# Prompt latent attention in a decode-step kernel: from one head per unit of 512 queries to two heads in the two row halves of TensorE's array, units of 256 queries

## The chip, the cores and the metric

The kernel runs on one core of one Trainium2 chip. The metric is the time of one launch on the device, in microseconds (us). TensorE is called PE below, its weight loads PEld, VectorE DVE, ScalarE ACT, GpSimd POOL, and SyncE (which issues most DMAs) SP. Each engine runs its own list of instructions in order, and the lists meet only at semaphores.

## The reference

One inference step of one layer of a hybrid decoder: a combined input projection, then three attention branches (latent, dilated windows, cross-attention to a memory), a SiLU gate and an output projection, for a prompt of 2048 tokens and for 64 sample tokens. The change touches only the latent attention of the prompt:

```python
def mla_prompt(q_lat, q_rope, ckv, krope):
    ...
    def block(args):
        ql, qr, start = args
        s = (jnp.einsum('bqhc,bkc->bhqk', ql, ckv)
             + jnp.einsum('bqhr,bkr->bhqk', qr, krope)) * MLA_SCALE
        qpos = start + jnp.arange(Q_BLOCK)
        p, _ = masked_softmax_stats(s, kpos[None, :] <= qpos[:, None])
        return jnp.einsum('bhqk,bkc->bqhc', p.astype(ckv.dtype), ckv)
```

There are 8 heads; the mask is causal. The kernel computes the same with keys and values expanded for each head: for a query, scores against keys of 64 "nope" numbers of its head and 32 rotary numbers that all heads share, a softmax, and a sum of values of 64 numbers per head. The scores have float32 accuracy.

## The kernel before

The program runs its stages one behind the other, with a barrier between them: input projection, prompt windows and memory, prompt latent projections, **prompt latent attention** (`prompt_latent_attention`, L1242), sample attention, output projection. The stage in question begins with a DMA issue at 764.94 us and its last matmul is at 1275 us.

Work is cut into 32 **units** (h, i): one head and 512 queries, the last 512 of a head first. A unit has four query blocks of 128. For each block the scores against all keys up to the diagonal are made in **score steps** of up to 512 keys (320 in all; `width` gives the keys). The steps of one unit:

- *Score* (L1411). Queries and keys are split into a high and a low part of the fast format (F32R), and three matmuls (hi x hi, hi x lo, lo x hi; L75 to L77 in `mm3`) add into one PSUM bank. Nope and rotary rows lie together, so a matmul uses 96 rows of the array. `scores` has two banks, so score step m waits until DVE has taken out step m-2.
- *Eviction* (L1552, operation at L1568). DVE copies the bank to `probs` with mask and scale, and keeps each row's minimum; behind the last step of a block a small reduce (L1573) gives `bias`.
- *Exponentials* (L1506, L1511). ACT works once over a block's whole row, up to 2048 columns, as soon as `bias` is there. They are issued on ACT when the next block's first score step comes.
- *Turn* (L1437). PE transposes `probs` in pieces of 64 x 128 in both row halves (lanes), two key blocks a turn, into one of two slots of `turned`. It waits until all exponentials of the unit are done. ACT copies lane 0 (L1513, L1519) and DVE lane 1 (L1576, L1583) to `probsT`.
- *Value* (L1453, L1463). Plain float32 matmuls of two key blocks against up to 512 columns of `probsT`, one key block in each column half (64 columns) of the array. A float32 matmul appears as two instructions in the trace. `outs` is double buffered.
- *Keep and back* (L1521, L1466, L1586). ACT copies `outs`, PE transposes it back (four transposes), DVE adds the two halves and scales with the reciprocal of the sums, and SP stores.

The order on PE, and with it on DVE and ACT (all three walk the same list `STEPS`), is fixed ahead by `phases()` and `order()` (L1263 to L1283): the phases are "two turns" and "[back of the unit before] two values" in turn, and before each phase score steps are put in until their share of the work is reached, with a lead of 15 us:

```python
        share = sum(0.705 * width(*s) / CH for s in SCORES) / sum(cost[what] for phase in phases() for what, u, p in phase)
...
            while m < len(SCORES) and (scored < share * (turned + LEAD) or m < unit_end[phase[-1][1]]):
```

`probs` has a buffer for each i, so four units can be in work. POOL splits the queries and keys of later units (L1386, L1394), and SP loads them ahead.

## Time and profile before

| | us |
|---|---|
| median of 3 runs (lowest, highest) | 2174.52 (2167.16, 2178.09) |
| the profiled execution's own time | 2173.66 |
| its span | 2172.0 |
| PE busy over the span | 2001.7 (92%) |
| DVE, ACT, POOL busy | 1132.3, 948.9, 416.6 |
| latent attention: first and last matmul start | 770.8, 1275.1 |

The span is the time between the first and the last instruction that the profiler saw; the execution's own time is that of the whole launch. Busy times are sums over instructions, and overlapping instructions of one engine count once. The ends of matmuls are modelled, so a start says more than an end.

### The profile page before, as it was taken

How to read it: one execution, taken by the hardware profiler on the slowest of the kernel's cores; microseconds unless marked ns; L12 is line 12 of the kernel's file. 1: busy time of each engine (PE TensorE's matmuls, PEld its weight loads, DVE VectorE, ACT ScalarE, POOL GpSimd, SP SyncE). 2: the span in 40 equal slices, each digit the busy share in tenths (PEclk: the TensorE clock that was granted, in tenths of full speed). 3: DMA queues.
4: the chain of work that ended last, by engine and by line, in shares of the span. 5: the costliest groups of instructions: out<-in, count | busy, mean ns of one | idle time of the engine just before them, and what ended most of it. 6: DMA issues, size and time to landing. Idle time of an engine off the chain costs nothing. (4 is left out here: it accounts for less than half of the span.)

```text
span 2172.0 us, 45434 instructions
## 1 busy us (share of the span) xinstructions
PE 2001.7 (92%) x16456; PEld 1470.0 (68%) x16456; DVE 1132.3 (52%) x3298; ACT 948.9 (44%) x2124; POOL 416.6 (19%) x530
## 2 busy tenths in 40 slices
PE   6999999688779979999999969999999969999998
PEld 5888887456557745555565545666666658888886
DVE  4333333577864357676776645555555663233222
ACT  4333332578752235555555434444444444243332
POOL 0111111344550022222221112222222100000000
PEclk9999999899999959999999989999999989999999
DMA  8333332623454321111110049877777353233231
GB/s 280 106 113 109 101 116 71 197 83 111 143 142 142 131 68 33 29 35 29 35 33 22 18 119 286 242 228 223 226 229 245 122 191 117 87 89 104 77 106 49
DMA packets 180293, 265.35 MB, mean 122 GB/s; under 512 B 44488, under 2 KB 138776, under 8 KB 171144
## 3 DMA queue, kind: packets, MB, share of 16 engines
q1 hardware_dynamic: 160712, 165.87, 27.1%
q0 software_dynamic: 19424, 97.35, 13.3%
q8 instruction: 102, 1.67, 0.3%
q14 instruction: 55, 0.45, 0.1%
HBM read 210.24 MB, written 52.66 MB: 121 GB/s over the span
## 5 line engine op out<-in xcount | busy, mean ns | idle before, releaser
L75 PE MATMUL proj_acc<-proj_w_hi,proj_x_hi 128*128 128x512 f32 (+2 forms) x544 | 197.6, 363 | 19.0 <-DVE proj_x_lo L299 12.4
L1511 ACT ACTIVATE mla_probs<-mla_probs,mla_bias 128x256 f32<-128x256 f32 (+14 forms) x128 | 154.7, 1209 | 109.2 <-DVE mla_bias L1573 104.5
L76 PE MATMUL proj_acc<-proj_w_lo,proj_x_hi 128*128 128x512 f32 (+2 forms) x544 | 195.9, 360 | 0.0
L77 PE MATMUL proj_acc<-proj_w_hi,proj_x_lo 128*128 128x512 f32 (+2 forms) x544 | 195.3, 359 | 0.0
L1568 DVE CUSTOM_DVE_ANT_0 mla_probs<-mla_scores,mla_zero 128x512 f32<-128x512 f32 x192 | 132.6, 692 | 112.0 <-PE mla_scores L77 108.1
L75 PE MATMUL mla_scores<-mla_k_hi,mla_q_hi 96*128 96x512 f32 (+3 forms) x320 | 143.4, 448 | 30.3 <-DVE mla_lowest L1568 14.5
L1463 PE MATMUL mla_outs<-mla_probsT,prompt_val 128*64 128x512 f32 (+3 forms) x640 | 141.1, 544 | 1.8 <-DVE mla_probsT L1583 1.8
L75 PEld LDWEIGHTS mla_scores<-mla_k_hi,mla_q_hi 96*128 96x128 f32 x320 | 62.5, 195 | 109.6 <-issue 62.6
L1917 PE MATMUL dec_outs<-late_ckv,dec_pT 128*64 128x256 f32 x1024 | 126.5, 389 | 3.7 <-DVE dec_pT L2047 3.7
L75 PEld LDWEIGHTS proj_acc<-proj_w_hi,proj_x_hi 128*128 128x128 f32 x544 | 104.0, 191 | 32.1 <-DVE proj_x_lo L299 12.4
L1862 PE MATMUL dec_scores<-dec_keysT,sample_q_lat 128*64 128x512 f32 x512 | 123.3, 601 | 2.2 <-DVE dec_krT L2025 1.2
L800 ACT ACTIVATE win_probs<-win_probs,win_bias 128x256 f32<-128x256 f32 (+1 forms) x256 | 117.4, 462 | 16.9 <-DVE win_bias L839 16.4
L76 PE MATMUL mla_scores<-mla_k_lo,mla_q_hi 96*128 96x512 f32 (+3 forms) x320 | 122.2, 382 | 0.0
L77 PE MATMUL mla_scores<-mla_k_hi,mla_q_lo 96*128 96x512 f32 (+3 forms) x320 | 121.8, 381 | 0.0
L353 DVE COPY proj_featT<-proj_tr 128x512 f32<-128x512 f32 x34 | 23.5, 692 | 187.8 <-PE proj_tr L406 186.0
L75 PE MATMUL fin_gate<-fin_wg_hi,fin_x_hi 128*128 128x512 f32 x272 | 109.0, 401 | 11.8 <-DVE fin_wg_lo L2340 8.1
L2047 DVE COPY dec_pT<-dec_p_turned 128x256 f32<-128x256 f32 x80 | 34.0, 424 | 159.7 <-PE dec_outs L1878 130.4
L1803 POOL DMA_INDIRECT late_ckv<-in_cache_ckv,sample_rows_of x63 | 59.8, 950 | 291.1 <-PE dec_outs L1917 278.6
L1519 ACT ACTIVATE mla_probsT<-mla_turned 128x512 f32<-128x512 f32 (+1 forms) x160 | 80.0, 551 | 79.4 <-PE mla_turned L1449 79.3
L77 PEld LDWEIGHTS proj_acc<-proj_w_hi,proj_x_lo 128*128 128x128 f32 x544 | 103.8, 191 | 12.9
L76 PEld LDWEIGHTS proj_acc<-proj_w_lo,proj_x_hi 128*128 128x128 f32 x544 | 103.8, 191 | 11.8
L77 PE MATMUL fin_gate<-fin_wg_hi,fin_x_lo 128*128 128x512 f32 x272 | 107.4, 395 | 0.0
(354 smaller groups left out, 4617.8 us busy)
## 6 DMA issues: line engine op xcount, KB each, us to landing
win_v_tile<-wv_out SPq DMA_DIRECT2D x75, 128.0 KB
proj_x_raw<-in_xT SPq DMA_DIRECT2D x17, 512.0 KB, 3.9
proj_rows<-in_x SPq DMA_DIRECT2D x17, 512.0 KB, 5.3
featT<-proj_featT POOLq DMA_DIRECT2D x34, 256.0 KB, 2.8
late_ckv<-in_xT SPq DMA_DIRECT2D x17, 512.0 KB, 6.8
fin_mix<-mix SPq DMA_DIRECT2D x17, 512.0 KB, 3.6
late_ckv<-in_x SPq DMA_DIRECT2D x17, 512.0 KB, 3.8
y_out<-late_ckv POOLq DMA_DIRECT2D x17, 512.0 KB, 6.5
```

What stands on the lines that cost most here:

```text
L75: pe.matmul(out, lh, rh, start=start, stop=False)
L76: pe.matmul(out, lh, rl, start=False, stop=False)
L77: return pe.matmul(out, ll, rh, start=False, stop=stop)
L800: e = act.activation(pr, pr, ACT.Exp, bias=bias[:, u, h:h + 1], scale=ATT_SCALE, accum_out=rec[:, q, 0, 256 + H_B + h:256 + H_B + h + 1])
L1463: mm = pe.matmul(outs[64 * kb:64 * kb + 64, u % 2, q0:], val[:, at, h, :], probsT[:, g % 2, kb, q0:], start=p == 0, stop=p == PAIRS[u] - 1)
L1511: act.activation(row, row, ACT.Exp, bias=bias[:, b_:b_ + 1], scale=-1.0, accum_out=total[:, b_:b_ + 1]).then_inc(exp_done, 1)
L1519: act.activation(dst, src, ACT.Copy).then_inc(turned_act, 1)
L1568: dve.tensor_tensor_reduce(probs[i][:, j, c * CH:c * CH + n], scores[:, m % 2, 0:n], add, -MLA_SCALE, -LOWEST, ALU.add, ALU.min, low).then ...
L1803: pool.indirect_dma_start(ckv[:, u, :, :].rearrange("p m c -> p (m c)"), None, ckv_rows, rows).then_inc(ckv_loaded[u], 16)
L1862: pe.matmul(scores[h * Q:(h + 1) * Q, u, :], q_lat[:, c, s, :], keysT[:, u, c, h * 512:(h + 1) * 512], start=c == 0, stop=False)
L1917: mm = pe.matmul(outs[h * Q:(h + 1) * Q, 0:KVL], pT[:, u, j, h * Q:(h + 1) * Q], values[:, h * HALF + j, :], start=j == 0, stop=j == HALF - 1)
L2047: dve.tensor_copy(pT[:, n % 2, :, 0:Q], halves_turned[0]).then_inc(pT_dve, 1)
```

## The change

Units are now (m, i): a **pair of heads** and **256 queries**, 32 in all; i runs up for even m and down for odd m. A score step serves both heads of the pair and there are 160. Head 2m lies in array rows 0 to 63, head 2m+1 in rows 64 to 127, so a step's matmuls use 64 rows each and come in pairs, one for each half. The shared rotary part no longer fits beside the nope part; it is packed as 32 rows of high and 32 rows of low part (`kr_parts`), with the rotary queries held twice. A step has five matmuls per head in place of three. `scores` has three banks, taken in turn by the heads of the steps. `probs` holds two units of any size. A value step has both heads on the column halves, two key blocks one behind the other, in one bank `outs` that is not double buffered any more; so `finish` needs no addition. The lead is 10 us and never more than one unit. The exponentials of both heads of a block are issued together. Loads have three DMAs for a unit's queries in place of two, and key chunks 1 to 3 of the first pair are split by ACT and DVE at units 1, 2 and 4. The core of the diff:

```diff
-    SB = 4
-    CH = SB * P
-    UNITS = [(h, i) for h in range(H_A) for i in reversed(range(SEQ // CH))]
+    QB = 2
+    CW = QB * P
+    CH = 512
+    NI = SEQ // CW
+    UNITS = [(m, i) for m in range(H_A // 2) for i in (range(NI) if m % 2 == 0 else reversed(range(NI)))]
     NU = len(UNITS)
-    LEAD = 15.0
+    LEAD = 10.0
...
+    STEPS_OF_SCORES = [(u, j, c) for u, (m, i) in enumerate(UNITS) for j in range(QB) for c in range(chunks(i, j))]
+    SCORES = [(u, j, c, s) for u, j, c in STEPS_OF_SCORES for s in range(2)]
+    PAIRS = [i + 1 for m, i in UNITS]
...
+        cost = {"turn": 0.58, "value": 0.95, "back": 0.25}
+        share = (sum(score_cost(k) for k in range(len(STEPS_OF_SCORES)))
+                 / sum(cost[what] for phase in phases() for what, u, p in phase))
+        k, scored, turned = 0, 0.0, 0.0
         for phase in phases():
-            turned += sum(cost[what] for what, u, p in phase)
-            while m < len(SCORES) and (scored < share * (turned + LEAD) or m < unit_end[phase[-1][1]]):
-                yield ("score", m, 0)
-                scored += 0.705 * width(*SCORES[m]) / CH
-                m += 1
+            u = phase[-1][1]
+            turned += sum(cost[what] for what, a, p in phase)
+            while k < len(STEPS_OF_SCORES) and k < unit_end[min(u + 1, NU - 1)] and (scored < share * (turned + LEAD) or k <= unit_end[u]):
+                yield ("score", k, 0)
+                scored += score_cost(k)
+                k += 1
             yield from phase
...
+        kr_parts = b.sb("kr_parts", [P, SEQ], F32R)
+        lower = b.sb("lower", [P, 1])
+        probs = b.sb("probs", [P, 2, 2 * QB, SEQ])
         probsT = b.sb("probsT", [P, 2, 2, CH])
-        outT = b.sb("outT", [P, 2, CH])
-        both = b.sb("both", [P, 2, SB, VH])
-        out = b.sb("out", [P, 2, SB, VH])
-        mask = b.sb("mask", [P, CH + P])
+        outT = b.sb("outT", [P, 2, CW])
...
-        scores = b.ps("scores", [P, 2, CH])
+        NR = NU * QB * 2
+        lowest = b.sb("lowest", [P, NR, SEQ // CH])
+        bias = b.sb("bias", [P, NR])
+        total = b.sb("total", [P, NR])
+        inv = b.sb("inv", [P, NR])
+        scores = b.ps("scores", [P, 3, CH])
         turned = b.ps("turned", [P, 2, 2, CH])
-        outs = b.ps("outs", [P, 2, CH])
+        outs = b.ps("outs", [P, CH])
...
+                parts = ((qn_hi[:, u % 2, mine], k_hi[:, m % 2, cols]), (qr_hi[:, u % 2, mine], kr_parts[:, cols]),
+                         (qn_hi[:, u % 2, mine], k_lo[:, m % 2, cols]), (qn_lo[:, u % 2, mine], k_hi[:, m % 2, cols]),
+                         (qr_lo[:, u % 2, mine], kr_parts[:, cols]))
+                for a, (lhs, rhs) in enumerate(parts):
+                    for s in range(2):
+                        at = 2 * k + s
+                        if a == 0 and at >= 3:
+                            pe.wait_ge(masked, at - 2)
+                        rows = slice(64 * s, 64 * s + 64)
+                        mm = pe.matmul(scores[:, at % 3, 0:n], lhs[rows, :], rhs[rows, :], start=a == 0, stop=a == len(parts) - 1)
+                        if a == len(parts) - 1:
+                            mm.then_inc(scores_done, 1)
...
+                pe.wait_ge(exp_done, 2 * QB * (u + 1))
...
-                if p == 0 and u >= 2:
-                    pe.wait_ge(out_kept, u - 1)
+                if p == 0 and u:
+                    pe.wait_ge(out_kept, u)
                 for kb in range(2):
                     at = 2 * p + kb
-                    q0 = max(0, at - SB * i) * P if i or at > 1 else 0
-                    mm = pe.matmul(outs[64 * kb:64 * kb + 64, u % 2, q0:], val[:, at, h, :], probsT[:, g % 2, kb, q0:], start=p == 0, stop=p == PAIRS[u] - 1)
+                    q0 = max(0, at - QB * i) * P
+                    for s in range(2):
+                        mm = pe.matmul(outs[64 * s:64 * s + 64, q0:CW], val[:, at, 2 * m + s, :],
+                                       probsT[:, g % 2, kb, s * CW + q0:(s + 1) * CW], start=at == 0, stop=at == 2 * PAIRS[u] - 1)
                 mm.then_inc(pv_done, 1)
...
-                for j in range(SB):
+                for j in range(QB):
...
+                    for s in range(2):
+                        if c == 0 and (u or j):
+                            exponentials(*((u, j - 1, s) if j else (u - 1, QB - 1, s)))
+                    if a == len(STEPS_OF_SCORES) - 1:
+                        for s in range(2):
+                            exponentials(u, j, s)
...
-                halves = turned[:, r % 2, 0, :].rearrange("p (j b d) -> p j b d", j=SB, b=2)
-                dve.tensor_copy(both[:, u % 2, :, :], halves[:, :, 0, :]).then_inc(added, 1)
-                dve.wait_ge(added, u + 1)
-                dve.tensor_tensor(both[:, u % 2, :, :], both[:, u % 2, :, :], halves[:, :, 1, :], ALU.add).then_inc(turned_dve, 1)
-                dve.wait_ge(turned_dve, r + 1)
-                dve.wait_ge(inverted, u + 1)
                 if u >= 2:
                     dve.wait_ge(stored[u % 2], 16 * (u // 2))
-                dve.tensor_tensor(out[:, u % 2, :, :], both[:, u % 2, :, :], inv[:, s].rearrange("p (j o) -> p j o", o=1).broadcast_to([P, SB, VH]), ALU.mult).then_inc(result_done, 1)
+                dve.tensor_tensor(out[:, u % 2, :, :, :].rearrange("p j s d -> p (j s) d"),
+                                  turned[:, r % 2, 0, 0:QB * P].rearrange("p (w d) -> p w d", d=VH),
+                                  inv[:, rows].rearrange("p (w o) -> p w o", o=1).broadcast_to([P, 2 * QB, VH]), ALU.mult).then_inc(turned_dve, 1)
```

Two places of the changed order. On **PE**, around the end of a unit's scores (in `scores` step order; `mla_turned<-mla_ident,mla_probs` are the turns). Before, 512 queries of one head:

```order
L1449 MATMUL mla_turned<-mla_ident,mla_probs 128x64 x32
L75 MATMUL mla_scores<-mla_k_hi,mla_q_hi 128x512
L76 MATMUL mla_scores<-mla_k_lo,mla_q_hi 128x512
L77 MATMUL mla_scores<-mla_k_hi,mla_q_lo 128x512
L75 MATMUL mla_scores<-mla_k_hi,mla_q_hi 128x384
L76 MATMUL mla_scores<-mla_k_lo,mla_q_hi 128x384
L77 MATMUL mla_scores<-mla_k_hi,mla_q_lo 128x384
L1471 MATMUL mla_turned<-mla_ident,mla_outT 128x128 x4
L1463 MATMUL mla_outs<-mla_probsT,prompt_val 64x512 x4
```

Now, the last score step of unit 9 (pair 1, i = 6, 256 keys), the first of unit 10 (512 keys), and the first turns of unit 9:

```order
L1474 MATMUL mla_scores<-mla_k_hi,mla_qn_lo 128x256 x2
L1474 MATMUL mla_scores<-mla_kr_parts,mla_qr_lo 128x256 x2
L1474 MATMUL mla_scores<-mla_k_hi,mla_qn_hi 128x512 x2
L1474 MATMUL mla_scores<-mla_kr_parts,mla_qr_hi 128x512 x2
L1474 MATMUL mla_scores<-mla_k_lo,mla_qn_hi 128x512 x2
L1474 MATMUL mla_scores<-mla_k_hi,mla_qn_lo 128x512 x2
L1474 MATMUL mla_scores<-mla_kr_parts,mla_qr_lo 128x512 x2
L1501 MATMUL mla_turned<-mla_ident,mla_probs 128x64 x32
L1525 MATMUL mla_turned<-mla_ident,mla_outT 128x128 x2
L1516 MATMUL mla_outs<-mla_probsT,prompt_val 64x256 x8
```

Scores stood between turns and values; here they stand ahead of the turns, and the turns of a unit follow one score step behind that unit's own last scores.

On **ACT**, the exponentials (`mla_probs,mla_total`) and the copies (`mla_probsT`). Before, around the longest row:

```order
L1511 ACTIVATE mla_probs,mla_total<-mla_probs,mla_bias 128x2048
L1519 ACTIVATE mla_probsT<-mla_turned 128x8x64
L1519 ACTIVATE mla_probsT<-mla_turned 128x2x2x64
L1511 ACTIVATE mla_probs,mla_total<-mla_probs,mla_bias 128x1152
L1525 ACTIVATE mla_outT<-mla_outs 128x512
```

Now, units 6 and 7 (i = 6 and 7 of pair 0):

```order
L1556 ACTIVATE mla_probs,mla_total<-mla_probs,mla_bias 128x1792 x2
L1564 ACTIVATE mla_probsT<-mla_turned 128x8x64 x4
L1556 ACTIVATE mla_probs,mla_total<-mla_probs,mla_bias 128x1920 x2
L1564 ACTIVATE mla_probsT<-mla_turned 128x8x64 x3
L1570 ACTIVATE mla_outT<-mla_outs 128x256
L1556 ACTIVATE mla_probs,mla_total<-mla_probs,mla_bias 128x2048 x2
L1564 ACTIVATE mla_probsT<-mla_turned 128x8x64 x6
```

One exponential at a time has become two in a row, and the copies behind the pair of 2048 columns are those of the unit to which that pair belongs.

## Rows read from the trace of the kernel before

**Rows 1.** Page, busy us of each engine over the span

```profile
PE 2001.7 (92%) x16456; PEld 1470.0 (68%) x16456; DVE 1132.3 (52%) x3298; ACT 948.9 (44%) x2124; POOL 416.6 (19%) x530
```

**Rows 2.** Stretches of the stage: busy us of PE, PEld, DVE, ACT, POOL; PEclk; DMA share; GB/s

```profile
770.70:806.40 35.70, 31.53 (x103) 22.32 (x104) 21.34 (x57) 14.89 (x18) 11.11 (x12) 0.50 0.20 52
785.00:795.00 10.00, 10.00 (x24) 6.82 (x24) 5.84 (x17) 4.66 (x4) 3.09 (x4) 0.50 0.00 0
850.00:1250.00 400.00, 387.44 (x3227) 238.05 (x3225) 282.42 (x846) 213.23 (x368) 86.45 (x92) 1.00 0.12 29
```

**Rows 3.** PE timeline of the stage: start us, length us, engine, line, tiles, shapes, count

```profile
1000.64 1.94 PE L1463 MATMUL mla_outs<-mla_probsT,prompt_val 128*64 128x512 f32 x8
1002.51 0.50 PE L75 MATMUL mla_scores<-mla_k_hi,mla_q_hi 96*128 96x512 f32 x1
1002.85 0.40 PE L76 MATMUL mla_scores<-mla_k_lo,mla_q_hi 96*128 96x512 f32 x1
1003.08 0.39 PE L77 MATMUL mla_scores<-mla_k_hi,mla_q_lo 96*128 96x512 f32 x1
1003.40 0.84 PE L1449 MATMUL mla_turned<-mla_ident,mla_probs 64*128 64x64 f32 x20
```

**Rows 4.** PE timeline in the windows stage (row halves of 64)

```profile
541.74 1.13 PE L735 MATMUL win_scores<-win_k_tile,win_q_tile 64*128 64x256 f32 x8
542.80 1.09 PE L751 MATMUL win_outs<-win_probsT,win_v_tile 128*64 128x128 f32 x16
```

**Rows 5.** PE timeline in the decode stage (column halves of 64)

```profile
1603.46 1.95 PE L1917 MATMUL dec_outs<-dec_v_rows,dec_pT 128*64 128x256 f32 x16
1605.24 1.89 PE L1862 MATMUL dec_scores<-dec_keysT,sample_q_lat 128*64 128x512 f32 x8
1606.95 1.04 PE L1866 MATMUL dec_scores<-dec_krT,sample_q_rot 128*64 128x128 f32 x16
```

**Rows 6.** Timeline around one eviction that the next scores wait for

```profile
858.61 0.40 PE L77 MATMUL mla_scores<-mla_k_hi,mla_q_lo 96*128 96x512 f32 x1
859.19 0.69 DVE L1568 CUSTOM_DVE_ANT_0 mla_probs<-mla_scores,mla_zero 128x512 f32<-128x512 f32 x1
859.81 0.28 DVE L1568 CUSTOM_DVE_ANT_0 mla_probs<-mla_scores,mla_mask 128x128 f32<-128x128 f32 x1
859.95 0.51 PE L75 MATMUL mla_scores<-mla_k_hi,mla_q_hi 96*128 96x512 f32 x1 [0.66 <-DVE mla_lowest L1568]
860.14 0.16 DVE L1573 TENSOR_REDUCE mla_bias<-mla_lowest 128x1 f32<-128x3 f32 x1
860.33 1.26 ACT L1511 ACTIVATE mla_probs<-mla_probs,mla_bias 128x1152 f32<-128x1152 f32 x1 [0.55 <-DVE mla_bias L1573]
```

**Rows 7.** Timeline, one exponential of 2048 columns and what follows on ACT

```profile
856.93 1.99 ACT L1511 ACTIVATE mla_probs<-mla_probs,mla_bias 128x2048 f32<-128x2048 f32 x1
858.92 0.86 ACT L1519 ACTIVATE mla_probsT<-mla_turned 128x512 f32<-128x512 f32 x2
```

**Rows 8.** Timeline of the stage's end: turns, copies, values, one back

```profile
1257.41 1.22 PE L1449 MATMUL mla_turned<-mla_ident,mla_probs 64*128 64x64 f32 x32
1258.16 1.29 DVE L1583 COPY mla_probsT<-mla_turned 128x512 f32<-128x512 f32 x2 [0.55 <-PE mla_turned L1449]
1259.00 1.94 PE L1463 MATMUL mla_outs<-mla_probsT,prompt_val 128*64 128x512 f32 x8 [0.38 <-DVE mla_probsT L1583]
1265.40 0.63 PE L1471 MATMUL mla_turned<-mla_ident,mla_outT 128*128 128x128 f32 x4 [0.37 <-DVE mla_probsT L1583]
```

**Rows 9.** Waits in the stage, turns for exponentials: us, times, longest

```profile
PEld mla_turned L1449 <- ACT mla_probs L1511: 0.8, 1, 0.8
```

**Rows 10.** Two stretches of the windows stage, one behind the other

```profile
437.80:441.30 3.50, 1.09 (x16) 0.88 (x16) 3.43 (x19) 2.14 (x9) 1.75 (x4) 1.00 0.14 44
441.30:444.70 3.40, 3.32 (x26) 2.44 (x26) 2.00 (x8) 2.37 (x9) 2.70 (x5) 0.50 0.09 30
```

**Rows 11.** Weight loads of one score group, PEld timeline

```profile
1002.61 0.19 PEld L76 LDWEIGHTS mla_scores<-mla_k_lo,mla_q_hi 96*128 96x128 f32 x1
```

More of the change, by code:

```diff
@@ L1360, in store @@
[L1360 to L1368 removed]
+                m, i = UNITS[u]
```

318 lines of the change are left out of this document (162 added, 156 removed).

## The prediction

> **What bounds the kernel now.** I read the page's busy times first: PE is busy for 2001.7 us of 2172.0, the next engine (DVE) for 1132.3 [rows 1]. Then the stretches of the one stage that the change touches: over 400 us of its middle PE is busy for 387.44, DVE for 282.42, ACT for 213.23, at a granted clock of 1.00 [rows 2]. So PE sets the pace there and what counts is PE's list: the length of its work and the gaps in it. From the first matmul to 806.40 us the granted clock is 0.50 (1.2 of 2.4 GHz), although PE was busy for all of 785 to 795 [rows 2]. The stage's PE time is 505 us (770.7 to 1276). Behind it come other stages that the change leaves alone, so a change of this time is the change of the kernel's.
>
> The 505 us add up as follows, which tests the prices used below. Scores: 140,288 key columns (the widths of the 320 steps) by three matmuls at 2400 columns/us are 175 us; a 512-column matmul starts 0.23 us behind the last (1002.85 to 1003.08 [rows 3]), 0.017 more than its columns, times 960: 16. Entering and leaving a group of score steps costs 0.11 + 0.09 us (first start to second 0.34, last to the turn 0.32 [rows 3]), times 150 groups: 30. Values: 80 phases of two at about 1.87 (1000.64 to 1002.51 [rows 3]), less for the diagonal ones, 130. Turns: 2192 transposes at 0.038 (1.22 us for 32 [rows 8]), 83. Backs: 32 at some 0.55 [rows 8], 17. That is 451; runs of three and more score steps, the slow clock at the start and the end's waits make up the rest.
>
> **What the change takes away on PE.**
> - Scores: 69,632 columns a head pair, five matmuls: 348,160 columns are 145 us if the two halves run side by side, and 800 pairs by 0.017 are 14. Together 159 in place of 192: **-33**. That the halves do run together rests on the nearest rows: in the windows stage eight instructions with 64 rows and 256 columns (four float32 matmuls, each two instructions of two passes, 0.213 us each) fill 1.06 us, 541.74 to 542.80 [rows 4], not the 1.70 that they need one by one; and less 0.16 for the change of shape, 0.225 us a pair.
> - Groups of score steps: 101 in place of 150, by 0.20: **-10**. Here the scores have the same 64-row shape as the turns, and all 101 groups touch a turn on one side. The extra 0.09 towards a turn was seen with a change from 96 to 64 rows [rows 3]; no row has the new pairing, so that side costs between 0 and 0.09, in all 9 us less or nothing less. I take 0.09, the row, and keep -9 as an end. The page TensorEngine Tiling (Array Packing) of the Trainium skill, section Key Properties, says that changing the tiling mode drains TensorE; by that page alone the side towards the turn would be free.
> - Values: as many columns, 256 wide in place of 512. Sixteen instructions of 256 columns take 1.78 us (1603.46 to 1605.24), eight of 512 take 1.71 [rows 5]: 72 double phases by 0.07, **+5**. Turns: 2180 transposes for 2192, nothing.
> - Backs: two transposes for four, half of 0.55 by 32 [rows 8]: **-8**.
> - DVE loses two operations of each `finish`. It is idle for 29% of the middle [rows 2], which covers them: nothing. POOL's splits and SP's loads are issued two units ahead; three DMAs in place of two for each unit stay behind that lead: nothing, up to +3 at the start if that cover is missing, as the first units are short.
>
> Sum of the work: **-46**.
>
> **What the change adds: waits.** I went through the planned order step by step with these prices.
>
> (A) *Score step behind score step.* Step k+1 writes for its second head the bank from which DVE takes step k's first head. From the start of the last matmul of a step (858.61, so its slot ends at 858.84) to the start of the eviction are 0.35 us, the eviction of 512 columns takes 0.69, and the next matmul starts 0.07 behind its end (859.95) [rows 6]. So PE stands for 1.1 us between two neighbouring steps, since matmuls go in order and the first head's later parts are behind the wait. In the old kernel, with one head per bank, two steps in a row were free, and only a third waited 0.42. The new order has 59 neighbours: 34 behind a step of 512 keys (1.10), 8 behind 384 (0.97), 3 behind 256 (0.83), 14 behind 128 (0.69), 57 us. In runs of three and more the first head gets ahead by one slot, 20 times 0.23 less: **+53**.
>
> (B) *Turns that wait for exponentials.* At units 6 to 10 and 22 to 26 one score step (one or two value steps besides at 6, 10, 22, 26) lies between a unit's last scores and its first turn, where the old order had many. The chain: 0.35 + 0.69 for the eviction, 0.16 reduce and its hand-over, 1.3 us in all before the first exponential can start [rows 6], then both heads' rows, of 2048 columns 2.0 + 0.1 us each (856.93 to the next ACT operation at 858.92 [rows 7]): 5.5 us. Against it stand the 1.1 of (A) and 1.15 of a step: 3.3 left, at four units. At the others, with 1792 and 1536 columns and ACT's keeping of `outs` in front where values lie between, it is 3.2, 2.8 and 2.8; 0.3 at units 11 and 27. Together 4 x 3.3 + 2 x (3.2 + 2.8 + 2.8 + 0.3): **+31**. Before, this wait came to 0.8 us in the whole stage [rows 9].
>
> (C) *Values straight behind their turns.* 32 times no score step lies between, 5 before. Two turns, then values: PE stands 0.4 us (1257.41 plus 32 transposes; DVE's first copy 1258.16; values at 1259.00 [rows 8]), which holds where DVE is free; where evictions are queued ahead of the copy, about 1.0; a single turn, which hides nothing of its own copy, about 1.0. I count 13 singles (12), 8 behind scores (8), 11 others (4): **+24**.
>
> (D) *Copies behind exponentials.* ACT has two exponentials in a row, up to 4.2 us, ahead of a turn's copy. Walking units 5 to 9 I find 0.2 to 1.6 us at four places a pair of heads and its mirror: **+8**.
>
> The old waits go: 52 third and fourth steps by 0.42, and 4 us at the end: **-26**. The start: before, 31.5 us of busy PE at half clock [rows 2] cost about 16, idle time 4; now the first units are short and wait a lot, so less of the work falls into the slow stretch. I take 12 in place of 20: **-8**.
>
> (E) *The clock in the middle.* In the windows stage a stretch with 1.09 us of PE work in 3.50 is followed by 3.40 us at 0.50 [rows 10]. The 10 long waits of (B), and runs such as the four of five neighbouring steps in units 2, 3, 18 and 19, are idle in the same way. A slow stretch of 3.4 us takes 1.7 us of PE's work away; 12 of them would be 20, part of it disappears in waits: **+10**, between 0 and 25.
>
> The sum: -46 + 53 + 31 + 24 + 8 - 26 - 8 + 10 = **+46**. Against the profiled execution's own 2173.66 that is 2220; the median of the runs, 2174.52, lies 0.9 above it, which I leave out. Forecast **2220**.
>
> **Rivals.**
> 1. *The waits hide one another* (not slower). In this case only the bank wait (A) is real, and exponentials, copies and clock (B to E, 73) fall into it or behind work, so that the saving wins: -46 + 53 - 26 - 8 = -27, **2147**. It decides when over 46 of the 73 vanish. For it speaks that a wait on two things is paid once and that ACT and DVE have 45% and 29% of slack [rows 2]. Against it: at the four longest waits the chain is ACT's own rows, 4.2 us, and there is nothing on PE to put over it. A part of it, with 20 to 46 hidden, ends between 2174 and 2200.
> 2. *The halves don't run side by side.* The page TensorE: Matmul & The Clock Gate of the Trainium skill, The mechanism in its Part 3, has a weight load overlap a matmul in flight only where the row group differs. By that each pair would also pay its loads. As a mechanism of this kernel: 800 pairs by a load's 0.19 us are 152, so **2370**. Against it: a load for the same 96 rows starts at 1002.61 [rows 11], within the matmul that starts at 1002.51 [rows 3], and the windows rows above. The trace does not agree with that rule, so it has a small chance.
> 3. *The clock stays low.* With PE idle for a quarter of the stage the slow stretches join up, as at the start, where 10 us of busy PE did not end them [rows 2]. A third of the 400 us of work at half speed, half of it hidden in waits, adds some 60: **2280**. Against it: at 806 it rose with the first turns and values, and these come every few us.
>
> **Chances and range.** Forecast 0.70; rival 1 0.19 (half of it below 2163), rival 2 0.03, rival 3 0.08. Ends of the forecast's terms: work -9 to +9, waits A to D 116 +/- 30, clock 0 to 25. That is 2180 to 2262. Downwards the range takes in the partial form of rival 1: **2172 to 2262**. A measurement of this kernel can tell about 0.5% (11 us) from no change. Faster by more 0.14, within 0.11, slower by more 0.75.
>
> **What the profile of the changed kernel would show.** Scores: pairs that start together, and pairs 0.23 us apart. (A): idle time of PE ahead of the second head's first matmul, released by DVE's eviction, some 55 to 60 times, near 1 us. (B): turns released by ACT's exponentials, ten waits of 2.5 to 3.5 us. (C, D): values released by the copies, some 30 us. PE busy in the stage's middle 75 to 80%, in place of 97%. (E): stretches of 0.50 around units 6 to 10. I am wrong if the stage's PE time is below 505 us; then B to D are to be read first. If it is above 600 us, the spacing of the score pairs.

## The result, and the profile after

| | before | after |
|---|---|---|
| median, us (lowest, highest) | 2175.59 (2167.16, 2178.09), 4 runs | 2240.40 (2234.45, 2243.45), 4 runs |
| profiled execution, its span | 2173.66, 2172.0 | 2238.77, 2236.9 |
| first matmul of the stage, last one | 770.8, 1275.1 | 778.45, 1342.3 |

The change makes the kernel slower: ratio **1.0283**, 95% interval [1.0259, 1.0307]. The spans differ by 64.9 us, and it lies in the stage: it begins 7.7 us later and takes some 58 us more from its first matmul on. The page of the changed kernel, busy PE beside [rows 1], and its row of granted clocks (40 slices):

```profile
PE 1981.5 (89%) x17532; PEld 1498.4 (67%) x17532; DVE 1097.8 (49%) x3222; ACT 938.3 (42%) x2112; POOL 395.5 (18%) x562
...
PEclk9999999899999869999798997999999989999999
```

PE is busy for 20 us less, although the time is 65 us more: the work did shrink, and more than that came back as idle time and, as shown below, as work at the lower clock. The whole stage, first of before, then of after (columns as in [rows 2]):

```profile
770.80:1276.00 505.20, 483.34 (x3920) 298.65 (x3920) 347.31 (x1026) 261.63 (x451) 110.70 (x118) 0.96 0.12 30
```

```profile
778.40:1342.00 563.60, 464.35 (x4994) 329.48 (x4994) 313.79 (x949) 250.46 (x438) 88.84 (x148) 0.89 0.11 30
```

The granted clock is a mean of stretches at 1.00 and at 0.50, so 0.89 over 563.6 us means 563.6 x 2 x 0.11 = 124 us at half clock; before it was 505.2 x 2 x 0.04 = 40, nearly all of it at the start [rows 2]. With two digits of the clock such a figure is good to some 5 us. Stretches of after show where it lies, the start and several in the middle:

```profile
790.00:806.00 16.00, 9.39 (x48) 6.22 (x48) 6.91 (x19) 5.16 (x12) 5.12 (x8) 0.50 0.11 35
...
900.00:1000.00 100.00, 85.08 (x958) 59.63 (x956) 57.76 (x167) 46.43 (x65) 8.57 (x16) 0.93 0.10 26
1050.00:1100.00 50.00, 38.47 (x342) 27.61 (x338) 22.94 (x81) 20.32 (x54) 10.25 (x20) 0.76 0.23 61
1150.00:1260.00 110.00, 93.02 (x1032) 64.88 (x1028) 60.10 (x175) 47.67 (x66) 8.55 (x16) 0.91 0.07 19
```

The stretches 900 to 1000 and 1150 to 1260 are about those of units 6 to 10 and 22 to 26; 1050 to 1100 is that of the short units between two head pairs, where no turn waits for exponentials.

The waits of after, in the rows of the weight loads (us, times, longest):

```profile
PEld mla_scores L1474 <- DVE mla_lowest L1615: 55.3, 57, 1.8
...
PEld mla_turned L1501 <- ACT mla_probs L1556: 30.6, 12, 3.3
...
PEld mla_outs L1516 <- ACT mla_probsT L1564: 16.7, 22, 1.8
...
PEld mla_scores L1474 <- DVE mla_bias L1615: 7.1, 8, 1.8
PEld mla_scores L1474 <- POOL mla_qr_lo L1430: 5.9, 2, 4.0
```

and in the rows of the matmuls, which count an idle time from the modelled end of the last matmul and so come out shorter:

```profile
PE mla_scores L1474 <- DVE mla_lowest L1615: 31.7, 44, 1.4
PE mla_turned L1501 <- ACT mla_probs L1556: 25.8, 10, 2.9
...
PE mla_outs L1516 <- DVE mla_probsT L1630: 14.7, 18, 1.8
PE mla_turned L1525 <- DVE mla_probsT L1630: 9.2, 11, 1.7
```

Read (A) in the first row of each list, (B) in the second, and (C) and (D) in the rows of `mla_outs` and of the backs. One place shows (A), (B) and the clock in a row, the last scores of unit 7 and the first turn (timeline):

```profile
942.71 0.39 PE L1474 MATMUL mla_scores<-mla_k_hi,mla_qn_hi 64*128 64x512 f32 x1
...
943.06 0.69 DVE L1615 CUSTOM_DVE_ANT_0 mla_probs<-mla_scores,mla_mask 128x512 f32<-128x512 f32 x1 [1.93 <-PE mla_scores L1474]
...
943.81 0.49 PE L1474 MATMUL mla_scores<-mla_k_hi,mla_qn_hi 64*128 64x512 f32 x1 [0.71 <-DVE mla_lowest L1615]
...
943.98 2.01 ACT L1556 ACTIVATE mla_probs<-mla_probs,mla_bias 128x2048 f32<-128x2048 f32 x1 [2.03 <-DVE mla_bias L1620]
...
945.99 1.99 ACT L1556 ACTIVATE mla_probs<-mla_probs,mla_bias 128x2048 f32<-128x2048 f32 x1
...
948.12 1.97 PE L1501 MATMUL mla_turned<-mla_ident,mla_probs 64*128 64x64 f32 x32 [2.88 <-ACT mla_probs L1556]
...
950.70 3.21 PE L1516 MATMUL mla_outs<-mla_probsT,prompt_val 128*64 128x256 f32 x16
```

The first head's first matmul is at 942.71. The second head's can only start at 943.81, 1.10 us later, when DVE has emptied its bank. The last matmul of the step starts at about 944.6, and the turn comes 3.5 us behind it, after two exponentials of 2.0 us. It then runs at half speed (32 transposes in 1.97 us, 1.22 in [rows 8]), and so do most of the values behind it (sixteen, busy for 3.21 us, where sixteen at 927.14 us are busy for 1.95).

### The profile page after: what moved, and what is told of

It is laid out like the page before. It is cut to its first block and busy times, and to the rows that moved or that the text cites. A ratio compares the mean times of both kernels' runs of the same rounds, so it can differ in the third digit from the quotient of the medians.

```text
span 2236.9 us, 47528 instructions
## 1 busy us (share of the span) xinstructions
PE 1981.5 (89%) x17532; PEld 1498.4 (67%) x17532; DVE 1097.8 (49%) x3222; ACT 938.3 (42%) x2112; POOL 395.5 (18%) x562
## 5 line engine op out<-in xcount | busy, mean ns | idle before, releaser
L1615 DVE CUSTOM_DVE_ANT_0 mla_probs<-mla_scores,mla_zero 128x512 f32<-128x512 f32 x192 | 124.9, 688 | 116.2 <-PE mla_scores L1474 116.1
L1556 ACT ACTIVATE mla_probs<-mla_probs,mla_bias 128x256 f32<-128x256 f32 (+15 forms) x128 | 152.6, 1195 | 59.6 <-DVE mla_bias L1620 54.8
L1516 PE MATMUL mla_outs<-mla_probsT,prompt_val 128*64 128x256 f32 (+1 forms) x1152 | 149.8, 404 | 20.1 <-DVE mla_probsT L1630 14.7
L1474 PE MATMUL mla_scores<-mla_k_hi,mla_qn_hi 64*128 64x512 f32 (+3 forms) x320 | 107.7, 470 | 61.3 <-DVE mla_lowest L1615 31.7
L1564 ACT ACTIVATE mla_probsT<-mla_turned 128x512 f32<-128x512 f32 x144 | 80.6, 596 | 183.5 <-PE mla_turned L1501 182.7
L1516 PEld LDWEIGHTS mla_outs<-mla_probsT,prompt_val 128*64 128x64 f32 x1152 | 85.2, 149 | 75.0 <-issue 34.3
L1630 DVE COPY mla_probsT<-mla_turned 128x512 f32<-128x512 f32 x144 | 94.1, 686 | 65.8 <-PE mla_turned L1501 63.8
L1501 PEld LDWEIGHTS mla_turned<-mla_ident,mla_probs 64*128 64x128 f32 x2180 | 88.3, 149 | 44.5 <-ACT mla_probs L1556 30.6
L1474 PEld LDWEIGHTS mla_scores<-mla_k_hi,mla_qn_hi 64*128 64x128 f32 x320 | 49.8, 201 | 101.3 <-DVE mla_lowest L1615 55.3
L1501 PE MATMUL mla_turned<-mla_ident,mla_probs 64*128 64x64 f32 x2180 | 94.6, 236 | 25.8 <-ACT mla_probs L1556 25.8
```

Source lines behind the costliest of these rows:

```text
L1474: mm = pe.matmul(scores[:, at % 3, 0:n], lhs[rows, :], rhs[rows, :], start=a == 0, stop=a == len(parts) - 1)
L1501: mm = pe.transpose(turned[:, r % 2, lane, (kb * 2 * QB + w) * 64:(kb * 2 * QB + w + 1) * 64], probs[rows, u % 2, w, src * P:(src + 1) * P ...
L1516: mm = pe.matmul(outs[64 * s:64 * s + 64, q0:CW], val[:, at, 2 * m + s, :], probsT[:, g % 2, kb, s * CW + q0:(s + 1) * CW], start=at == 0, ...
L1556: act.activation(row, row, ACT.Exp, bias=bias[:, at:at + 1], scale=-1.0, accum_out=total[:, at:at + 1]).then_inc(exp_done, 1)
L1615: dve.tensor_tensor_reduce(probs[:, u % 2, w, c * CH:c * CH + wide], scores[:, n % 3, 0:wide], add, -MLA_SCALE, -LOWEST, ALU.add, ALU.min, ...
L1630: dve.tensor_copy(dst, src).then_inc(turned_dve, 1)
```

## The experiments

Ratios are to the kernel before, timed beside each experiment. Microseconds gained or lost against the changed kernel are worked out from two such ratios, unless they are called readings of a profile.

### E1: fill the waits for exponentials

```diff
+                if p == 0 and u in (6, 7, 8, 9, 10, 22, 23, 24, 25, 26):
...
+                    pe.wait_ge(masked, 2 * nxt - 2)
+                    for _ in range(8):
+                        pe.matmul(scores[:, (2 * nxt) % 3, 0:CH], k_hi[:, mk % 2, 0:P], k_hi[:, mk % 2, 0:CH], start=True, stop=True)
                 pe.wait_ge(exp_done, 2 * QB * (u + 1))
```

> The changed kernel with eight matmuls of 128 rows by 512 columns (1.8 us at the full clock) put on TensorE ahead of the turns that wait for exponentials, at units 6 to 10 and 22 to 26, into the score bank that is written next. They compute nothing that is used and take no wait away; they only keep the array at work during waits of 2.5 to 3 us. Theory 1 (long waits cost twice, since half clock follows them, term E): the half-clock stretches between 900 and 1000 us and around 1150 to 1260 us go, the kernel gains 8 to 20 us on the changed kernel's 2240, ratio to before 1.019 to 1.025. Rival (the clock falls for other reasons, or what it takes disappears in waits): within 3 us of 2240, ratio 1.027 to 1.030, or slower where the filling runs at half clock and outlasts the wait.

Measured: **1.0231** [1.0202, 1.026]. The stage:

```profile
778.40:1321.20 542.80, 459.46 (x5076) 328.23 (x5076) 313.30 (x949) 249.84 (x438) 88.60 (x148) 0.95 0.11 31
```

80 useless matmuls make the kernel faster by 0.5% (11 us). The profiled execution was the fastest of the four, and its stage is 20.8 us shorter, so its clock shows rather more than the median. The half-clock time falls from 124 to 542.8 x 2 x 0.05 = 54 us. The waits for the lowest scores stay (32.4 us, 31.7 without the filling). In the stretches of the ten turns the clock is now full:

```profile
900.00:1000.00 100.00, 91.81 (x1034) 64.71 (x1030) 60.18 (x174) 47.89 (x70) 8.55 (x16) 1.00 0.11 28
1150.00:1260.00 110.00, 101.72 (x1130) 71.73 (x1126) 65.11 (x189) 51.93 (x73) 9.72 (x18) 1.00 0.06 16
```

So term (E) is real: 100 x 2 x 0.07 + 110 x 2 x 0.09 = 34 us at half clock hung on the idle time ahead of these turns. The other half of the 70 lies elsewhere, at the start and around 1050 to 1120, where nothing was filled; this run doesn't show what took it away.

### E2: exponentials of half the length

```diff
-                row = probs[:, u % 2, w, 0:key_blocks(UNITS[u][1], j) * P]
-                act.activation(row, row, ACT.Exp, bias=bias[:, at:at + 1], scale=-1.0, accum_out=...)
+                n = key_blocks(UNITS[u][1], j) * P
+                row = probs[:, u % 2, w, (n // 2 if n > 1024 else 0):n]
+                act.activation(row, row, ACT.Exp, scale=-1e-4, accum_out=...)
```

> The changed kernel in which the exponentials of rows longer than 1024 columns work on their last half only (the first half keeps raw scores, and all exponentials run without their bias and with a small scale: this part of the softmax is left out). It halves the chain of term B without touching TensorE's list. Theory 1 (turns wait for the two exponentials of the last block, term B): TensorE's waits for exponentials fall from 26 us in ten places to 8 us or less, copies behind exponentials (D) shrink too, and less half clock follows: 20 to 35 us faster than 2240, ratio 1.012 to 1.020. Rival (the exponentials are only the last of several things awaited, and another wait takes their place): under 8 us.

Measured: **1.0132** [1.0114, 1.015], 33 us less than the changed kernel, inside what my theory expected. The turns' waits in the rows of the matmuls:

```profile
PE mla_turned L1501 <- ACT mla_probs L1557: 9.3, 10, 1.2
```

16.5 us of wait went, to 9.3 us where I had expected 8 or less; the waits of values for DVE's copies stayed (14.7 us, as before). The rest of the 33 I put down to the clock, which is 0.93 over a stage of 532.2 us in place of 0.89 over 563.6, so 75 us at half clock in place of 124. As in E1 it is 1.00 from 900 to 1000 and from 1150 to 1260, while from 1060 to 1120 it is 0.74 in both kernels. So (B) with the clock that hangs on it is about half of what the change lost, and the slow stretch between the head pairs has another cause.

### E3 and E4: another order of the same steps

The score steps of the next unit are dealt out evenly over a unit's phases in E3; in E4 the last two phases of a unit get none, so that more work lies between a unit's last scores and its first turn.

```diff
-            while k < len(STEPS_OF_SCORES) and k < unit_end[min(u + 1, NU - 1)] and (scored < share * (turned + LEAD) or k <= unit_end[u]):
...
+            steps = unit_end[min(u + 1, NU - 1)] - k
+            for n, phase in enumerate(mine):
+                due = -(-steps * (n + 1) // slots) if n < slots else steps
+                while k < unit_end[u] + due:
```

(`slots` is the number of the unit's phases in E3, and two fewer in E4 for units with more than four.)

> The changed kernel with another order of the same steps: the score steps of unit u+1 are spread evenly over the gaps in unit u's phases, before turns and between turns and values alike. Neighbouring score steps fall from 59 to 14, turns straight before values from 32 to 11. But one score step ahead of a unit's first turn is all that stands between last scores and turns at every unit, so the waits for exponentials (B) grow to nearly all units with i of 2 and more, by 20 to 30 us. Theory 1 (A, 1.1 us for each neighbour, is the largest term): -45 (A) - 12 (C) + 25 (B) - 5 (clock) = 35 us faster than 2240, 2190 to 2220. Rival (A is mostly covered, B is the main cost): B's growth shows alone, 2250 or slower.

> As the even order, but the last two gaps of a unit's phases (for units with more than four) get no score steps, so that five to seven us of work stand between a unit's last scores and its first turn. Neighbouring score steps 38 (59 in the change), turns straight before values 21 (32). Theory 1: A -23, C -8, B -20 or better, clock -10: 2170 to 2190. If B were not real the result would lie behind the even order (it has 24 more neighbours, 26 us): 2215 to 2245. If it is faster than the even order, the waits for exponentials cost more than the neighbours.

Measured: **1.0118** [1.0096, 1.014] and **1.0084** [1.0056, 1.0111]. E3's waits, then E4's:

```profile
PE mla_turned L1504 <- ACT mla_probs L1559: 42.6, 25, 3.1
PE mla_outs L1519 <- DVE mla_probsT L1633: 24.3, 26, 2.6
...
PE mla_scores L1477 <- DVE mla_lowest L1618: 12.0, 18, 1.8
```

```profile
PE mla_scores L1477 <- DVE mla_lowest L1618: 31.1, 38, 1.8
PE mla_turned L1504 <- ACT mla_probs L1559: 24.1, 21, 2.7
PE mla_outs L1519 <- DVE mla_probsT L1633: 20.2, 28, 2.6
```

With 14 neighbours in place of 59, (A) falls to 12.0 us from 31.7, and (B) grows to 42.6; with a gap (A) is back at 31.1 and (B) is 24.1. E3 lies where I expected it. E4 has 2196 us where I expected 2170 to 2190, and the intervals of the two overlap, so they don't decide which wait costs more. They take 36 and 43 us off the changed kernel with the same matmuls, so more than half of the loss is one of order. They trade one wait for another: neither has enough score steps apart from each other and enough cover for the exponentials.

### E5: both heads in the same row half

```diff
-                        rows = slice(64 * s, 64 * s + 64)
+                        rows = slice(0, 64)
```

> The changed kernel with both heads' score matmuls read from array rows 0 to 63 (the second head computes the first head's scores, so the output of the odd heads is another's). The number, the sizes and the order of all instructions stay; only the two matmuls of a pair can no longer run side by side. Theory (the halves do run together, which is where the 33 us of the saving come from): 800 pairs by 0.213 us are 159 us more on TensorE, of which waits for evictions take up some 10 to 30: 2360 to 2395 in place of 2240, ratio to before 1.085 to 1.10, and matmuls of a pair 0.23 us apart. Rival (they never overlapped): 2240, nothing changes.

Measured: **1.13** [1.1267, 1.1332], 221 us more than the changed kernel and well above the 1.085 to 1.10 that I expected. Pairs of 512 columns in this kernel (timeline):

```profile
1009.05 0.62 PE L1474 MATMUL mla_scores<-mla_kr_parts,mla_qr_hi 64*128 64x512 f32 x2
1009.51 0.62 PE L1474 MATMUL mla_scores<-mla_k_lo,mla_qn_hi 64*128 64x512 f32 x2
```

and in the changed kernel:

```profile
958.42 0.40 PE L1474 MATMUL mla_scores<-mla_kr_parts,mla_qr_hi 64*128 64x512 f32 x2
958.66 0.40 PE L1474 MATMUL mla_scores<-mla_k_lo,mla_qn_hi 64*128 64x512 f32 x2
```

0.46 us a pair in one half, 0.23 in two: the halves run side by side in full, and rival 2 falls. What goes beyond the expected 159 us (62 us, and more if waits took up some of it) I put down to the clock, which no run separates here: over the 774.6 us of this stage it was 0.77, with long stretches at half clock although PE was busy, as

```profile
1158.80:1210.00 51.20, 46.40 (x228) 35.27 (x229) 16.00 (x58) 14.35 (x41) 8.47 (x16) 0.50 0.13 31
```

### E6 and E10: the late start

The first matmul came 7.7 us later than before. In the changed kernel (timeline: SP's issue, ACT's first key rounding, the first matmul):

```profile
767.22 0.60 SPq L1379 DMA_DIRECT2D mla_probs<-featT  x1
...
776.28 0.63 ACT L1549 ACTIVATE mla_k_hi<-mla_k_raw 128x512 fp32r<-128x512 f32 x1 [3.49 <-DMA mla_probs<-featT]
...
778.45 0.47 PE L1474 MATMUL mla_scores<-mla_k_hi,mla_qn_hi 64*128 64x128 f32 x2 [19.66 <-DVE mla_kr_parts L1599]
```

The first chunk of rotary keys needs 9 us from issue to use. E6 holds back the loads behind it; E10 loads the same bytes of the first unit, rotary keys and rotary queries, in plain transfers.

```diff
+            sp.wait_ge(first_k_loaded[0], 32)
             load_q(1)
```

```diff
-                sp.dma_start(kr_raw(c), rows.rearrange("(o r) t -> o r t", o=1).broadcast_to([4, ROPE, CH])).then_inc(first_k_loaded[c], 16)
...
+                    for g in range(4):
+                        sp.dma_start(probs[32 * g:32 * g + 32, 1, 0, SEQ - CH:], rows).then_inc(first_k_loaded[0], 16)
```

> The changed kernel; SyncE waits until the first key chunk has landed before it issues the queries of unit 1 and the key chunks 1 to 3. In the changed kernel's profile the first matmul of the stage starts at 778.45 us (770.8 before) and the first rotary chunk takes 9 us from issue to landing. Theory 1 (the loads issued behind it share the DMA engines and hold it up): the first matmul starts 3 to 6 us earlier and the kernel gains 2 to 5 us, unless later chunks come too late and units 2 to 4 wait. Rival (the loads of the first unit are slow in themselves, by their form: rows read again for two or four copies): the first matmul stays at 778 and the kernel is the same or up to 5 us slower.

> The changed kernel, and for the first unit the rotary queries are loaded by two transfers of 32 rows a head, the first chunk of rotary keys by four transfers of 32 rows, in place of one transfer each that repeats its source rows (the same bytes to the same places; 5 more issues of some 0.5 us). Theory 1 (the form of the repeated transfer is what takes 9 us from issue to landing, where the old kernel's 64 KB chunk took 2.6): the first K rounding on ACT, at 776.3 before, comes at 772 to 773.5, the first matmul of the stage at 774 to 776, and the time falls by 2 to 5 us, ratio 1.026 to 1.027. Rival (it is the bytes, 256 KB where the old kernel moved 64, with queries, keys and mask ahead of or beside them, or the same source rows read four times): landing no earlier, the first matmul at 778 to 781, ratio 1.028 to 1.030.

E6: **1.0306** [1.027, 1.0342], first matmul still at 778.42. The later loads aren't the cause. E10: **1.0267** [1.021, 1.0324]; its timeline:

```profile
766.13 1.82 SPq L1387 DMA_DIRECT2D mla_probs<-featT  x4
...
769.87 0.63 ACT L1557 ACTIVATE mla_k_hi<-mla_k_raw 128x512 fp32r<-128x512 f32 x1 [2.08 <-DMA mla_probs<-featT]
...
772.03 0.48 PE L1482 MATMUL mla_scores<-mla_k_hi,mla_qn_hi 64*128 64x128 f32 x2 [14.98 <-DVE mla_kr_parts L1608]
```

3.7 us from the first issue to use, and each transfer lands 2.3 us after its issue (median). PE is idle 14.98 us ahead of the stage in place of 19.66, so the form of the loads costs 4.7 us; the rest of the earlier start is that SP began 1.7 us sooner in this execution (763.42 in place of 765.15), which is also why rounding and first matmul come some 2 us earlier than I expected. The interval of the time is too wide to show 4.7 us (0.2%); the trace does. How busy the 16 DMA engines are hints at the reason. While the changed kernel waits for its repeated rows their share is 0.27, which is about what four of the 16 would give, and with the plain transfers it is up to 0.87 (the last but one number of a row, the changed kernel first, then E10). Which engines a transfer used isn't in the traces.

```profile
775.00:776.00 1.00, 0.00 (x0) 0.00 (x0) 0.00 (x0) 0.00 (x0) 0.00 (x0) 0.50 0.27 99
...
767.00:768.00 1.00, 0.00 (x0) 0.00 (x0) 0.41 (x2) 0.72 (x2) 0.00 (x0) 0.50 0.87 295
```

### E7 and E8: exponentials ahead of the next value step

ACT gets the exponentials of a block ahead of the next value step or first turn, in place of ahead of the next block's evictions. E7 uses E4's order, E8 E3's.

```diff
...
+                elif what == "value":
+                    flush()
...
```

> The even order with its last two gaps empty, and in addition ScalarE issues the exponentials of a block ahead of the next value step (before it keeps the sums), in place of at the next block's first score step. TensorE's and VectorE's lists are those of the even order with gaps. There, 24 us of waits of turns for exponentials are left in 21 places, since ScalarE's list has the exponentials behind the copies and behind the keeping of outs. Theory (B is a question of when the chain can begin): these waits fall to 8 us or less, 10 to 18 us faster than the even order with gaps (2196): 2178 to 2186, ratio to before near 1.00. Rival (the exponentials then stand ahead of the copies of the next turns and hold up the values, term D): within 5 us of 2196.

> The even order without gaps, with the exponentials issued ahead of the next value step as in the run before it. TensorE has 14 neighbouring score steps (38 with gaps). Left of B: the chain of 5.5 us against two value steps and a score step, 3 us, at the longest rows: 1 to 2.4 us at units with i from 4 to 7, some 25 us in place of 43. Theory: 12 to 20 us faster than the even order (2205): 2185 to 2193. If it is faster than the gap version, the neighbours (A) cost more than the rest of B.

E7: **1.0213** [1.018, 1.0245], slower than E4 where faster was expected. Its longest wait:

```profile
PE mla_outs L1519 <- ACT mla_probsT L1567: 37.7, 17, 3.4
```

The wait of the turns is gone (1.8 us are left) and came back as (D): ACT's copies stand behind two exponentials of up to 2 us, and the values wait for them, 2.2 us each. That is the rival of this run, and stronger than it was stated. E8: **1.0067** [1.004, 1.0094]; 0.5% below E3, less than expected. Waits for exponentials fell from 42.6 to 21.9 us. In these two orders early exponentials pay only where few values follow directly behind their turns (11 times in E8, 21 in E7).

### E9: filling in the better order

E4 with eight, six and four useless matmuls ahead of the twelve turns that waited longest.

```diff
+                if p == 0 and u % 16 in {9: 8, 11: 6, 12: 4, 13: 4, 14: 4}:
...
```

> The order of e4_even_gap, and ahead of the first turn of units 9 and 25 eight added 128x512 matmuls (results unused, into a score bank that is free), six at 11 and 27, four at 12 to 14 and 28 to 30. In the profile of e4_even_gap these twelve turns waited for exponentials for 1.2 to 2.7 us each, 19 us together. My theory (slow stretches start from such waits): the waits turn into PE work of the same length, the stretches of granted clock 0.50 behind them get fewer, and the time falls by 3 to 8 us against e4_even_gap, so a ratio of 1.005 to 1.007 to the kernel before. Rival (in this order the waits of 1 to 3 us are too short or too rare to lower the clock, and its half-clock time comes from the start and from score steps in a row): no change within 2 us, ratio 1.008 to 1.009, or a few us longer where eight or four matmuls last beyond the wait. The first matmul of the stage stays at 778 us.

Measured: **1.0054** [1.0028, 1.008], inside the range of my theory, but its interval overlaps that of E4 [1.0056, 1.0111], so this run alone doesn't settle it. Clock over the stage 0.96 in place of 0.94.

### E12 and E11: a table of steps

What E3, E4 and E7 showed is that four waits must be kept small together. So I searched the order with the prices from the rows (pairs, turns, values, 0.69 for eviction and copy, the exponential by its columns), swapping neighbouring steps as long as the sum of work and waits fell, and wrote the result as a table: how many score steps stand ahead of each other step.

```diff
+    AHEAD = ("312110010101012101000112010100100120100111100102010001110010013010100100010001020100001100110010"
...
-            while k < len(STEPS_OF_SCORES) and k < unit_end[min(u + 1, NU - 1)] and (scored < share * (turned + LEAD) or k <= unit_end[u]):
...
+        for n, (what, u, p) in enumerate(step for phase in phases() for step in phase):
+            for _ in range(int(AHEAD[n])):
+                yield ("score", k, 0)
+                k += 1
+            yield what, u, p
```

E12 has the table, the early exponentials and plain loads for all units; E11 the table and the early exponentials alone.

> The changed kernel with three edits: the place of each score step is written out in a table (searched with the prices of waits A to D read from the traces; 23 score steps stand straight behind another in place of 59, 11 values straight behind their turns in place of 32, and 3 to 4 us of work between a unit's last scores and its first turn at the long units); the exponentials are issued as early as in e8_even_early; the rotary queries and keys are loaded by transfers of 32 rows each, as in e10_plain, for all units and the four first chunks. My theory (what the change loses is the waits A to D, the clock that falls with them, and the start, and all of it is order): waits of PE for lowest scores 15 to 22 us, for exponentials under 8, values for copies 5 to 15, half-clock stretches well under the 89 us of the changed kernel, first matmul at 771 to 774 us; stage's PE time 470 to 495 us in place of 564, and a time 5 to 30 us below the kernel before: ratio 0.986 to 0.998. Rival (with fewer score steps in a row there are more groups, 137 in place of 101, and the waits only move, as they did from exponentials to copies in e7_gap_early): the ratio stays at 1.003 to 1.010, and the wait rows add up to 60 us or more.

> e12_table_plain with the loads of the changed kernel again (one transfer that repeats its rows): only the table of steps and the early exponentials are left of its edits. It tells which of the two took the time from e8_even_early (1.0067) to e12_table_plain (0.9782). Theory 1 (the order): the loads are worth what e10_plain showed at the start, 5 to 7 us, so the first matmul is at 777 to 779 us again, the waits of PE for lowest scores, exponentials and copies stay at 20 to 35 us together, and the ratio is 0.980 to 0.984. Rival (the loads count in all units, since they also hold POOL's splits and so the first scores of the next unit): waits for POOL's splits of 10 us or more, ratio 0.987 or above.

E12: **0.9782** [0.9761, 0.9803], median 2131.43 us beside 2180.76 of the kernel before: **faster than both kernels**, and further than I expected (0.986 to 0.998, a stage of 470 to 495 us). E11: **0.985** [0.9801, 0.99], just above my range, with the waits for POOL's splits between the two theories. E12's stage and its waits:

```profile
771.70:1231.00 459.30, 426.02 (x4996) 299.79 (x4996) 314.18 (x949) 249.26 (x438) 88.73 (x148) 0.97 0.14 38
```

```profile
PE mla_scores L1474 <- DVE mla_lowest L1625: 19.9, 24, 3.9
...
PE mla_outs L1516 <- DVE mla_probsT L1640: 4.2, 6, 0.9
PE mla_scores L1474 <- POOL mla_qr_lo L1430: 2.7, 2, 2.5
PE mla_turned L1501 <- ACT mla_probs L1556: 2.0, 3, 0.9
```

The stage takes 459.3 us in place of 563.6, with the same matmuls and the same number of score steps. The half-clock time is down to 459.3 x 2 x 0.03 = 28 us, and all of it lies before 840 us (the clock is 1.00 from there on). The slow stretch between the head pairs is gone too, though no run says which wait had made it. E11 has the same waits but for POOL's splits (7.5 us in place of 2.7), a stage of 465.5 us and 19.5 us of idle PE ahead of it (15.0 in E12). So the loads are worth 6.2 + 4.5 = 11 us in the traces (15 us by the ratios, whose intervals just overlap). The rest, from 1.0283 to 0.985 or 94 us, is the table with the early exponentials; the two weren't run apart. The loads matter more than the 5 to 7 us that I expected; 4.8 us of the 6.2 are the waits for POOL's splits.

Would a better order alone have brought the old kernel as far? That wasn't run. Its waits in the stage, the start left out, are these:

```profile
PE mla_scores L75 <- DVE mla_lowest L1568: 14.5, 24, 2.4
...
PE mla_scores L75 <- DVE mla_bias L1568: 2.6, 8, 0.3
PE mla_outs L1463 <- DVE mla_probsT L1583: 1.8, 3, 0.7
...
```

With two rows of backs (1.1 and 0.7) that is 20.7 us, where E12 is 49 us faster. To these come what its 40 us at half clock cost (at most 20, nearly all at the start) and whatever fewer groups of score steps would save, so it isn't shown that the old kernel couldn't come near E12. What speaks for the packing is the work, 51 us less by the estimate below.

## Why the prediction was right

Forecast 2220 (2172 to 2262), slower at 0.75; measured 2240.4, slower. The sum was +46, the traces give +65. The mechanism is the forecast one: less work, more waits, on PE's own list. But the 19 us between the two sums are a remainder of larger errors that partly cancel. The two rows of the whole stage show it. By the forecast PE's busy time there changes by -46 - 8 + 10 = -44 and its idle time by 116 - 26 = +90; measured are -19 and +77 (99.3 in place of 21.9). So busy time is 25 us above the forecast, idle time 13 below, and the start 7.7 above.

- **Work, -46: right, somewhat too small.** Take off half of the half-clock time, and PE's busy time in the stage was 483 - 20 = 463 before, and is 426 - 14 = 412 in E12, which has all the changed kernel's matmuls and few waits: -51, an estimate to some 5 us (from the starts of the matmuls alone I get -57). Pairs are 0.23 us apart, sixteen value instructions take 1.87 us (927.14 to 929.01). The side of a group towards a turn, which I took at 0.09 with -9 as an end, is free here; the turn follows the last matmul by 0.23, its columns' time:

```profile
924.44 0.40 PE L1474 MATMUL mla_scores<-mla_kr_parts,mla_qr_lo 64*128 64x512 f32 x2
924.67 1.15 PE L1501 MATMUL mla_turned<-mla_ident,mla_probs 64*128 64x64 f32 x32
```

- **(A) +53: right.** 57 waits of 55.3 us for lowest scores in the rows of the loads, 7.1 more for `bias`; 1.10 us at 942.71. E3 took 45 of the 59 neighbours away and the waits fell with them.
- **(B) +31: right**: 30.6 us in the rows of the loads, 25.8 in ten waits in those of the matmuls, 2.88 at the longest. E2 shows that it costs more than its own length, because the clock hangs on it.
- **(C) and (D), +32: right in sum.** The matmul rows for values and backs behind copies give 14.7 + 9.2 and some 3 of ACT's, 27 us. How it divides between the two can't be read from them; that (D) is a mechanism of its own E7 shows.
- **(E) +10 and the start's -8: mis-sized.** This is the term that was furthest off. Together I had +2 for the clock. If the work is 46 to 51 us less, PE's busy time should be 432 to 437 us, and it is 464: the lower clock stretches it by some 27 to 32 us more than before. That fits 84 us more at half clock, which can cost 42 at most. I had counted twelve stretches of 3.4 us, from [rows 10]. Behind the waits of (B) they came much like that (34 us, E1 and E2). What I had not foreseen is the rest: the 50 us from 1050 alone hold 50 x 2 x 0.24 = 24 us of half clock, without any wait of (B). And the slow start, which ended at 806 in [rows 2], now reaches beyond it: 0.50 to 806 and 44 x 2 x 0.24 = 21 us more up to 850 (granted clock 0.76 there).
- **The start, 0 to +3: wrong.** It cost 7.7 us. I had said that the loads stay behind a lead of two units, which is no argument for the first unit, and I counted transfers, not their form: the repeated transfers are 4.7 us of it (E10). The other 3 I put down to more issues and two more operations ahead of the first matmul (`kr_parts` on ACT and DVE); no run takes them away.

Two signs came otherwise than I had written: PE is busy for 84% of the middle (379 of 450 us from 850 to 1300) in place of 75 to 80%, as slow work counts as busy, and the slow stretches are not only around units 6 to 10. That the forecast is within 1% of the measured time is in part luck: too little for the clock and the start (33 to 38 us) stands against too much waiting and too little saving (13 to 18).

Rival 1, that the waits hide one another, didn't happen in the changed order: the five rows of the loads shown above add up to 116 us, the sum of my terms (A) to (D). The match is closer than it deserves, since 5.9 of it are waits for POOL, for which I had nothing, and the copies that DVE makes are missing from it. Its time, 2147, is near what the packing gives once the waits are ordered away, but by another way: E12 has 2131. Rival 2 falls with E5. Rival 3, slow stretches that join up for +60, was half right: there is more half clock than I took in the sum, and it costs less than it said.

## What to carry to other kernels

When a change makes a step serve two tiles at once, its buffers come free in pairs and its consumers get work in pairs: cost each neighbour of such steps by the chain through the other engine (here 1.1 us), not by the slack of the engine. Before dropping a change that lost to waits, keep its matmuls and re-order the steps by the prices that the trace gives; here the same matmuls took 459 us in place of 564. And a long wait of PE can cost twice, once as a wait and once at half clock behind it (E1, E2), so remove the longest waits first; a start needs its own sum, since no lead covers it.

## What the runs showed of the hardware that I had not expected

- A transfer that repeats 32 source rows into 128 partitions (256 KB) was used 9 us after its issue, four plain ones of 64 KB each with the same bytes 3.7 us after the first issue (E10).
- 80 matmuls whose results nobody reads made the kernel 11 us faster, and the granted clock in the stretches where they stand rose from 0.93 and 0.91 to 1.00 (E1).
- PE at half clock while busy for 46.4 of 51.2 us (E5), where its score matmuls used one row half.
